# Six of the norms' means as four rounded products of a split sum of squares, half a chunk later in TensorE's order

## What is computed

```python
def _rmsnorm(x, g):
    xf = x.astype(jnp.float32)
    y = xf * lax.rsqrt(jnp.mean(xf * xf, axis=-1, keepdims=True) + EPS)
    return (y * g.astype(jnp.float32)).astype(x.dtype)
...
def _mem_attn(h, mk, mv, w_q, q_norm, w_o):
    bsz, t, _ = h.shape
    q = _rmsnorm((h @ w_q).reshape(bsz, t, X_HEADS, X_HEAD_DIM), q_norm)
...
        x = x + _mem_attn(_rmsnorm(x, p["g_x"][l]), mem_k[l], mem_v[l], p["w_xq"][l],
                          p["x_q_norm"][l], p["w_xo"][l])
        val, g = jnp.split(_rmsnorm(x, p["g_ffn"][l]) @ p["w_up"][l], 2, axis=-1)
```

## Time and profile before

| | us |
|---|---|
| time, median of 3 runs (1587.42 to 1590.53) | 1588.78 |
| profiled execution, first to last instruction (span) | 1586.5 |
| PE busy | 1568.0 (99%) |
| DVE busy | 976.5 (62%) |
| POOL busy | 637.4 (40%) |
| ACT busy | 623.3 (39%) |

### The profile page before, as it was taken

One profiled execution on the slowest core, in us unless ns is written; L12 is line 12 of the kernel. 1 busy time (PEld: TensorE's weight loads), 2 busy tenths in 40 slices (PEclk: granted clock), 3 DMA queues, 4 the chain that ended last, 5 costly groups with the idle time before them and its releaser, 6 DMA issues.

```text
span 1586.5 us, 30727 instructions
## 1 busy us (share of the span) xinstructions
PE 1568.0 (99%) x11884; PEld 1492.3 (94%) x11886; DVE 976.5 (62%) x1394; ACT 623.3 (39%) x923; POOL 637.4 (40%) x305
## 2 busy tenths in 40 slices
PE   8999999999999999999999999999999999999999
PEld 7889848997999999999999998999799999999999
DVE  7799885764665564555657878766466553055530
ACT  6332474334443332333335675434434332133321
POOL 4345522330434343343435667532143434334342
PEclk9999999999999999999999999999999999999999
DMA  5342421240322232222323333224022222222222
GB/s 203 133 146 95 134 74 41 94 173 14 106 94 79 93 99 76 91 79 93 98 80 100 113 104 117 98 93 160 21 87 89 82 98 92 76 93 79 97 92 94
DMA packets 42390, 153.86 MB, mean 97 GB/s; under 512 B 5632, under 2 KB 6656, under 8 KB 41032
## 3 DMA queue, kind: packets, MB, share of 16 engines
q1 hardware_dynamic: 42312, 152.75, 28.9%
HBM read 145.53 MB, written 9.30 MB: 98 GB/s over the span
## 4 chain that ended last, share of the span: by engine, by line
PE 85%; DVE 6%; issue 3%; POOL 3%; ACT 2%; DMA 0%; POOLq 0%; SPq 0%; ACTq 0%; DVEq 0%
PE PS L963 75%; POOL WLO L471 3%; PE AX L1294 2%; PE AX L963 2%; PE PS L1262 1%; DVE SC L1535 1%; PE AX L1187 1%; PE PS L1200 1%; PE PS L1300 0%; DVE XL L1475 0%; PE AX L1030 0%; PE AX L1220 0%; DVE RSTD L1435 0%; PE AX L1162 0%; PE AX L1262 0%
## 5 line engine op out<-in xcount | busy, mean ns | idle before, releaser
L471 POOL TENSOR_TENSOR WLO<-WRAW,WHI 128x1024 fp32r<-128x1024 f32 (+3 forms) x301 | 637.2, 2126 | 933.7 <-ACT WHI L502 933.6
L502 ACT ACTIVATE WHI<-WRAW 128x1024 fp32r<-128x1024 f32 (+3 forms) x301 | 268.8, 913 | 602.7 <-PE PS L963 571.4
L963 PE MATMUL PS<-XH,WHI 128*128 128x272 f32 (+1 forms) x2128 | 444.3, 290 | 3.4 <-DVE XL L1475 2.6
L963 PE MATMUL PS<-XH,WLO 128*128 128x272 f32 (+1 forms) x2128 | 440.1, 288 | 0.0
L963 PE MATMUL PS<-XL,WHI 128*128 128x272 f32 (+1 forms) x2128 | 437.7, 287 | 0.0
L963 PEld LDWEIGHTS PS<-XH,WHI 128*128 128x128 f32 x2128 | 337.4, 188 | 11.3 <-POOL WLO L471 5.8
L963 PEld LDWEIGHTS PS<-XL,WHI 128*128 128x128 f32 x2128 | 337.1, 188 | 0.0
L963 PEld LDWEIGHTS PS<-XH,WLO 128*128 128x128 f32 x2128 | 335.2, 188 | 0.0
L963 PE MATMUL PS<-HH,WHI 128*128 128x272 f32 x1216 | 253.9, 290 | 0.1
L963 PE MATMUL PS<-HL,WHI 128*128 128x272 f32 x1216 | 251.1, 287 | 0.0
L963 PE MATMUL PS<-HH,WLO 128*128 128x272 f32 x1216 | 251.0, 287 | 0.0
(11 more groups left out here) (285 smaller groups left out, 1755.1 us busy)
## 6 DMA issues: line engine op xcount, KB each, us to landing
WRAW<-in_w_in_even SPq DMA_DIRECT2D x29, 512.0 KB, 3.3
WRAW<-in_w_up0a SPq DMA_DIRECT2D x22, 512.0 KB, 3.2
WRAW<-in_w_up0b SPq DMA_DIRECT2D x22, 512.0 KB, 3.2
WRAW<-in_w_up1a SPq DMA_DIRECT2D x22, 512.0 KB, 3.2
WRAW<-in_w_up1b SPq DMA_DIRECT2D x22, 512.0 KB, 3.2
WRAW<-in_w_mv SPq DMA_DIRECT2D x16, 512.0 KB, 3.3
WRAW<-in_w_xq SPq DMA_DIRECT2D x16, 512.0 KB, 3.3
WRAW<-in_w_xo SPq DMA_DIRECT2D x16, 512.0 KB, 3.3
```

The costliest lines, as they stand in the source:

```text
L471: pool.tensor_tensor(WLO[parity][:, first:last], WRAW[parity][:, first:last], WHIf[parity][:, first:last], ALU.subtract).then_inc(lo_done, ...
L502: act.activation(WHI[parity][:, first:last], WRAW[parity][:, first:last], ACT.Copy).then_inc(hi_done, 2 // len(cuts))
L963: ins = pe.matmul(dst, w, x, start=first, stop=last)
```

## The change

The mean of six norms (heads 0 and 1 of both cross-attentions, and the norms in front of both `up a`) is taken in another way. SQA is split: ACT copies it, rounded, into the first half of a new tile SQR (`sum_rounded`), DVE subtracts that from SQA into the second half (`sum_rest`), and PE multiplies both halves by a rounded matrix of ones ONR, four fp32r products that add up in the same PSUM bank (`split_mean`). ONR holds 1/1024, which is a power of two; for heads the root multiplies by 4. SQR lies where SQ lies, ONR in a part of CST that nothing read; ACT writes ONR once, early. The six means also move: from behind chunk 2 and chunk 4 of `xq` to the middle of chunk 3 and chunk 5, and from behind chunk 0 of `up a` to the middle of chunk 1. The other means stay as they were.

```diff
+SPLIT_SUMS = [("h", 0), ("h", 1), ("n", 2), ("h", 4), ("h", 5), ("n", 5)]
...
+            def sum_rounded(use):
+
+                kind, n = use
+                if use in SPLIT_SUMS:
+                    act.wait_ge(*((sq_summed, 8 * n + 8) if kind == "n" else (hn_sum, n + 1)))
+                    act.activation(SQR[:, 0, :], SQA[:], ACT.Copy).then_inc(sum_high, 1)
...
+                               scale=float(D // 256) if ("h", u) in SPLIT_SUMS else 1.0).then_inc(hn_std, 1)
...
+            act.wait_ge(cst_landed, 32)
+            act.activation(ONR[:], ONES_D, ACT.Copy)
             ahead(c0 + 2)
...
                     head_square(u0 + hd, QX[:, 2 * hd:2 * hd + 2, :], t0 + 2 * hd + 2)
+                    sum_rounded(("h", u0 + hd))
...
+                if half == "a":
+                    sum_rounded(("n", READS[ph]))
                 ahead(c0)
...
                     chunk(c0 + m, (c0 + m) % 2, t0 + m, (t0 + m) % 2, kt, rh, rl, ready if m == 0 else None, base,
-                          first_cut=HP if m % 2 == 0 and ph[0:2] == "up" else H)
-                    if m == 0 and behind_first:
-                        behind_first()
+                          halfway=in_second if m == 1 else None, first_cut=HP if m % 2 == 0 and ph[0:2] == "up" else H)
...
+            def split_mean(use, at_, done):
+
+                pe.wait_ge(sum_low, SPLIT_SUMS.index(use) + 1)
+                for n in range(2):
+                    for i in range(2):
+                        ins = pe.matmul(AX[:, at_ + i, 0:H], ONR[:], SQR[:, n, i * H:(i + 1) * H],
+                                        start=n == 0, stop=n == 1)
+                ins.then_inc(done, 1)
...
-                    chunk(c0 + m, (c0 + m) % 2, t0 + m, (t0 + m) % 2, KT, XH, XL, xl_ready if m == 0 else None, 8 * norm)
+                    chunk(c0 + m, (c0 + m) % 2, t0 + m, (t0 + m) % 2, KT, XH, XL, xl_ready if m == 0 else None, 8 * norm,
+                          halfway=(lambda: head_mean(u0 + m // 2 - 1)) if m in (3, 5) else None)
                     if m == 0:
                         mean_square(norm)
-                    if m in (2, 4, 6):
-                        head_mean(u0 + m // 2 - 1)
+                    if m == 6:
+                        head_mean(u0 + 2)
...
+            def sum_rest(use):
+
+                if use in SPLIT_SUMS:
+                    dve.wait_ge(sum_high, SPLIT_SUMS.index(use) + 1)
+                    dve.tensor_tensor(SQR[:, 1, :], SQA[:], SQR[:, 0, :].bitcast(F32), ALU.subtract).then_inc(sum_low, 1)
```

More of the change, by code:

```diff
@@ L210, in build @@
         RSTD, PR, CST, CQ, CSTB, RM, RMC, SP, NSP, SPT, HB, GQ, FST, AST, CSTATE, HST, STAT, WARM = pack(C_AT, M_AT, consts)
-        IDENT, ONES_D, ONES_X, ONES_B = (CST[:, 128 * i:128 * i + 128] for i in range(4))
+        IDENT, ONES_D, ONES_X = (CST[:, 128 * i:128 * i + 128] for i in range(3))
         SPREAD, SPREAD_K, MEAN_Q, MEAN_K = CQ[:, 0:128], CQ[:, 128:256], CQ[:, 256:288], CQ[:, 288:320]
@@ L217, in build @@
         SQ, SQA, STD = pack(S_AT, END, [("SQ", [P, 2, T], F32), ("SQA", [P, T], F32), ("STD", [P, T], F32)])
+        SQR = at("SQR", [P, 2, T], F32R, S_AT)
+        ONR = at("ONR", [P, P], F32R, C_AT + sum(size(s, d) for _, s, d in consts[:2]) + 3 * P * 4)
         S2 = S_AT + size([P, 2, T], F32) + 2 * tile_b
@@ L306, in build @@
                                                          sem("mk_read"), sem("mk_out"))
+        sum_high, sum_low = sem("sum_high"), sem("sum_low")
         hn_sq, hn_sum, hn_mm, hn_std, hn_out = sem("hn_sq"), sem("hn_sum"), sem("hn_mm"), sem("hn_std"), sem("hn_out")
@@ L538, in head_std @@
                 at_ = query_mean_at(u)
-                act.activation(halves(STD[:]), AX[:, at_:at_ + 2, 0:H], ACT.Sqrt, bias=par("eps")).then_inc(hn_std, 1)
+                act.activation(halves(STD[:]), AX[:, at_:at_ + 2, 0:H], ACT.Sqrt, bias=par("eps"),
+                               scale=float(D // 256) if ("h", u) in SPLIT_SUMS else 1.0).then_inc(hn_std, 1)
             def residual(ph):
@@ L724, in cross @@
                 c0, u0, t0 = C0[f"xq{l}"], HN0[f"xq{l}"], T0[f"xq{l}"]
+                sum_rounded(("n", READS[f"xq{l}"]))
                 ahead(c0)
@@ L996, in chunk, with linear @@
                 ins.then_inc(chunk_done, 1)
-            def linear(ph, kt, rh, rl, ready, base, behind_first=None, woven=False):
+            def linear(ph, kt, rh, rl, ready, base, in_second=None, woven=False):
                 c0, t0, n = C0[ph], T0[ph], LEN[ph]
@@ L1010, in linear @@
                               first_cut=HP if k == 0 and ph[0:2] == "up" else H)
+            def split_mean(use, at_, done):
[5 more added lines that the diff above has]
+                ins.then_inc(done, 1)
             def mean_square(norm):
-                pe.wait_ge(sq_summed, 8 * norm + 8)
                 if HN_BEFORE[norm]:
                     pe.wait_ge(hn_std, HN_BEFORE[norm])
+                if ("n", norm) in SPLIT_SUMS:
+                    split_mean(("n", norm), 0, ssq_done)
+                    return
+                pe.wait_ge(sq_summed, 8 * norm + 8)
                 for i in range(2):
@@ L1028, in head_mean @@
                     pe.wait_ge(xexp, 4 + 20 * (u // 4))
+                if ("h", u) in SPLIT_SUMS:
+                    split_mean(("h", u), at_, hn_mm)
+                    return
                 for i in range(2):
@@ L1737, in cross @@
                 c0, t0, u0 = C0[f"xq{l}"], T0[f"xq{l}"], HN0[f"xq{l}"]
+                sum_rest(("n", READS[f"xq{l}"]))
                 rstd(READS[f"xq{l}"])
@@ L1799, in cross @@
                         maximum(0)
+                    sum_rest(("h", u0 + hd))
                 maximum(1)
@@ L1820, in ffn_up @@
                 if half == "a":
+                    sum_rest(("n", READS[ph]))
                     link(dve.memset(GB[:, 0:4], 0.0))
```

## The result

The changed kernel takes 1592.49 us (median of 13 runs, 1587.82 to 1596.56), the kernel before 1587.61 in the same session: a ratio of 1.0024 with a 95% interval of 1.0014 to 1.0034. A second session gave 1590.42 against 1588.58, and a ratio of 1.0016 (1.0006 to 1.0027); one run of 3090.8 us is left out of that median, which is 1591.04 with it. Ratios and intervals here are taken over all the fast runs of a session and are not the quotient of two medians (1592.49 over 1587.61 would be 1.0031). The forecast was 1589.3, +0.5 us and no measured difference, with a range up to 1592.0. The medians lie 1.8 and 4.9 above those of before, the first of them 0.5 above the range, and the ratio lies on either side of 0.2%.

A forecast was written before the change was run, and what follows sets the result against it. PE was taken to bound the kernel (85% of the chain). Heads -1.7 and `up a` norms +2.2, with nothing for ONR, gave +0.5 us on 1588.78, so 1589.3 us; range 1585.9 to 1592.0.

The forecast's parts named there:

- The price of a mean: On PE, four rounded products take 0.50 us instead of 0.92 for two fp32 products, saving 0.42 per mean.
- the chain of `up a`: Two norms: root and everything behind it 1.1 us later, PE waits about 1.65 before chunk 3; +2.2 us in all.
- the part of the heads: Four head means in `xq` stay on PE's own path and save 4 x 0.42, -1.7 us.
- the walk from head 0's root to head 1's split: In `xq`, head 1's split is ready at 330.4, 1.5 us before PE asks in the middle of chunk 5.
- if PE waits in the middle of chunk 5: Sign in `xq` that the forecast is wrong; PE was to pass there without idle time.
- Slack in the chain of `up a`: Rival, chance 0.15: the chain has unseen slack, so all six means give 0.42; -2.5 us, 1586.3.
- The clock in `up a`: Rival, chance 0.09: PE's new gap before chunk 3 brings half clock, 1.7 us more per layer; +3.9, 1592.7.
- The table load: Rival, chance 0.05: ACT's table load in `up a` waits for the mean too, 1.28 per chain; +3.1, 1591.9.
- the rounded mean is cheaper: Opposite of a rival, chance 0.06: the rounded mean still takes 0.92 on PE; +3.0 us, 1591.8.
- The half clock in the cross-attention: Rival, chance 0.10: the half-clock stretch moves; one less gives 1587.6, one more 1591.0.

The follow-up runs named there:

- e3: The changed kernel with all six split means placed behind block 2 of 8 of the chunk instead of block 4: 1589.10 us against 1588.68 before, ratio 0.9999.
- e8: e3 with ACT rounding the weights of chunks 3 and 5 of `up a` earlier: 1586.94 us against 1588.58 before, ratio 0.9993.

## Where the prediction was right and where it was wrong

The number came out near: +0.5 us and no measured difference were forecast, and the change costs about +2.8 us of work, 0.18%. That it looks near is partly luck of scale: the term that failed was off by 2.4 us, and that is only 0.15% of this kernel's time. The price of a mean and the chain of `up a` were right as mechanisms, the part of the heads was not.

**The price of a mean was right.** The chain gives four products 0.51, and in e3 two means give 0.83 per cross. The rows of tile SQR (count, then shortest, median and longest in ns) show that none of the six subtractions was held. ONR was not tried alone.

```profile
L1034 PE MATMUL AX<-SQR,ONR x24: 284/288/367, 321.5 to 1201.2; 128*128 128x272 f32 x24
...
L1462 DVE TENSOR_TENSOR SQR<-SQA,SQR x6: 726/726/727, 317.7 to 1197.7; 128x544 fp32r<-128x544 f32 x6
```

**The norms were right.** The root follows PE's mean, not the table load, and stands 3.70 behind the end of chunk 0 (1197.83 to 1201.53; predicted 3.7) instead of 2.65:

```profile
1197.83 0.41 PE L982 MATMUL PS<-XH,WHI 128*128 128x272 f32 x2
...
1200.84 0.66 PE L1034 MATMUL AX<-SQR,ONR 128*128 128x272 f32 x4
...
1201.53 0.72 ACT L539 ACTIVATE STD<-AX,PR 128x544 f32<-128x544 f32 x1 [1.06 <-PE AX L1034]
...
1209.05 2.78 POOL L476 TENSOR_TENSOR WLO<-WRAW,WHI 128x1024 fp32r<-128x1024 f32 x1 [7.34 <-ACT WHI L507]
```

The waits of PE, total, times and longest: two new ones of 1.4 before chunk 3 (some 1.6 were predicted), and the old two of 0.4 as they were. The wait of 0.5 at head 3's mean (L1062) is new too, where none was forecast.

```profile
PE AX L982 <- POOL WLO L476: 2.8, 2, 1.4
...
PE AX L1062 <- DVE SQA L1494: 1.1, 2, 0.5
...
PE PS L982 <- POOL WLO L476: 0.8, 2, 0.4
```

WLO of chunk 3 ends 14.00 behind the end of chunk 0 (1209.05 + 2.78 - 1197.83) instead of 12.97 (1203.52 - 1190.55), and that of chunk 5 is late by the same 1.03: +1.1 was predicted for each.

**The step that failed is "stay on PE's own path: 4 x 0.42 = -1.7 us"**, and in its working the walk from head 0's root to head 1's split. It moved the eviction of chunk 3 by 2.6 us and priced the sum by a POOL that "now is" idle, but it left out the scalings that stand between the reciprocal and that eviction. Moved by 2.6 they start at 324.5, and WLO, 0.42 earlier than in the earlier trace rows, at 324.3: so the trace of before (321.88 above, and the earlier trace rows) already told of the collision, and the rows that the prediction quoted leave the scalings out. Head 1's split was then ready at 334.14, 0.13 behind the moment at which PE could have gone on, where the walk had it 1.5 us ahead. The Trainium skill, "SBUF — State Buffer", section "Who interferes with whom", has the rule that was needed (a DVE instruction with two SBUF inputs is locked out for the whole of a GpSimd instruction that reads SBUF); it was applied to the added subtractions, none of which was ever held, and not to the instructions that were only moved. The trace agrees with it by 3.60 against 1.48. The term came out as 2 x 0.36 = +0.7 instead of -1.7, and the sum as +2.8 instead of +0.5. The sentence that was to catch it did: "if PE waits in the middle of chunk 5".

**The rivals.** Slack in the chain of `up a` is refuted by the waits. The clock in `up a` stayed at 1.00 (eighth column) behind PE's new gap, which ends at 461.63 in layer 0; PE was busy for 13.20 of these 15 us:

```profile
460.00:475.00 15.00, 13.20 (x103) 12.76 (x103) 10.79 (x17) 6.36 (x8) 6.37 (x3) 1.00 0.22 70
```

The table load ran ahead of the mean, and the rounded mean is cheaper. The half clock in the cross-attention did vary, but from run to run of one kernel, and with the same mean clock as before.

## What to carry to other kernels

When a step moves, move every instruction behind it up to the next wait, and lay each one over the other engines' timeline; the instructions that the diff doesn't name collide as well as those that it adds. An instruction placed "early enough" for its consumer can still be late for a window that another engine is about to close: here 1.5 us in PE's order (middle of the chunk against block 2) were worth 4 us of work, 2.4 of it in the cross-attentions (2 x (0.36 + 0.83)) and the rest in the chain of `up a`. And where runs differ by stretches of clock, compare time times granted clock beside the medians.

## What the hardware showed that was not expected

The stretches at half clock vary between runs of one program, and nothing here tells what sets them: the runs of e8 lay at mean clocks of 0.994 to 0.999, those of the changed kernel at 0.995 to 1.000, and the changed kernel's profiled run spent about 6.8 us at half clock in each cross-attention (a mean of 0.66 over the 10 us from 380), its repetition none. Two windows of those, the changed kernel and then its repetition (granted clock in the eighth column):

```profile
381.00:384.00 3.00, 3.00 (x17) 3.00 (x17) 0.04 (x1) 0.00 (x0) 0.00 (x0) 0.51 0.00 0
```

```profile
381.00:384.00 3.00, 2.88 (x10) 1.39 (x9) 0.35 (x1) 1.75 (x2) 2.02 (x1) 1.00 0.01 3
```

Five stretches are an estimated 8.5 us (5 x 1.7); whether the kernels with 0.9970 (e3, e8) lose a little more than before's 0.9977 to 0.9980 stays open. And a DVE copy of two columns with one SBUF input is held like the operations with two: 2.38 us for one that takes 0.17. It was there to be read before any run: in the kernel before, the copy ahead of the history write of chunk 2 runs into WLO of chunk 4 and takes 2.02, in the serial chain that leads to WLO of chunk 5.

```profile
1206.71 2.39 POOL L471 TENSOR_TENSOR WLO<-WRAW,WHI 128x1024 fp32r<-128x1024 f32 x1 [3.19 <-ACT WHI L502]
1207.11 2.02 DVE L1828 COPY FST<-GB 128x2 f32<-128x2 f32 x1
```

The Trainium skill, "SBUF — State Buffer", section "Who interferes with whom", says that copies can take the shared ports too, where their operands meet its conditions; the trace agrees by 2.38 against 0.17.
